# x scaled by its norm on VectorE before it is turned, and the columns of three modulations moved

## What is computed

```python
h = modulate(rms_norm(x, g_pre), shift, scale)   # h * (1 + scale) + shift
y = sublayer(h)
x = x + gate * rms_norm(y, g_post)
```

## Time and profile before

| | |
|---|---|
| median of 3 runs | 1044.78 us (1044.73 to 1045.03) |
| profiled execution, its own time | 1045.76 us |
| its span in the profile | 1044.0 us |
| busy share: PE, PEld, DVE, ACT, POOL | 98%, 86%, 75%, 52%, 7% |
| HBM read | 239.30 MB, 230 GB/s over the span |
| granted TensorE clock, mean | 0.996 |

### The profile page before, as it was taken

The page is one execution under the profiler, slowest core; times in us unless marked ns, Lnnn a source line. Parts: engine busy times, 40 slices in busy tenths (PEclk is TensorE's granted clock), DMA queues, the critical chain, the costliest instruction groups (busy, mean ns, idle before and its releaser), DMA issues.

```text
span 1044.0 us, 17276 instructions
## 1 busy us (share of the span) xinstructions
PE 1020.3 (98%) x7098; PEld 898.2 (86%) x7099; DVE 785.7 (75%) x1162; ACT 538.5 (52%) x706; POOL 74.8 (7%) x79
## 2 busy tenths in 40 slices
PE   6999999999999999999999999999999999999997
PEld 3677799889988999887989899899999689999995
DVE  2457798768878888866968778761787689878786
ACT  4443644344446457765545445454763565544543
POOL 0000000000000000000720000000790000000000
PEclk9999999999999999999999999999999999999999
DMA  9999699887997997003988777723344277555511
GB/s 339 384 369 353 220 348 357 316 318 279 336 330 258 277 376 287 1 5 125 390 300 314 273 285 281 228 86 117 122 141 158 67 249 235 168 196 185 179 41 41
DMA packets 131226, 243.56 MB, mean 233 GB/s; under 512 B 6521, under 2 KB 97228, under 8 KB 125004
## 3 DMA queue, kind: packets, MB, share of 16 engines
q1 hardware_dynamic: 126640, 238.77, 65.1%
q10 hardware_dynamic: 4507, 3.69, 1.3%
HBM read 239.30 MB, written 1.05 MB: 230 GB/s over the span
## 4 chain that ended last, share of the span: by engine, by line
PE 86%; DVE 6%; DMA 2%; ACT 2%; SPq 2%; issue 1%; DVEq 0%; ACTq 0%
PE bank L1898 24%; PE bank L1830 13%; PE bank L1832 12%; PE bank L1831 12%; PE bank L1910 3%; PE bank L1741 2%; DVE wlo L1135 2%; PE bank L1786 1%; SPq L607 1%; PE bank L2175 1%; DMA raw<-in_b_w_in_dram 1%; PE bank L2201 1%; DMA raw<-in_ada_w_dram 1%; PE bank L1768 1%; PE bank L1844 1%
## 5 line engine op out<-in xcount | busy, mean ns | idle before, releaser
L1135 DVE TENSOR_TENSOR wlo<-raw,whi 128x2048 fp32r<-128x2048 f32 (+1 forms) x145 | 331.5, 2291 | 60.0 <-ACT whi L674 58.4
L674 ACT ACTIVATE whi<-raw 128x2048 fp32r<-128x2048 f32 (+1 forms) x145 | 274.9, 1897 | 143.9 <-PE bank L1898 80.5
L1830 PE MATMUL bank<-hcat,whi 128*128 128x256 f32 x1096 | 313.2, 286 | 2.6 <-DVE wlo L1135 2.6
L1831 PE MATMUL bank<-hcat,whi 128*128 128x256 f32 x1096 | 310.7, 284 | 0.0
L1832 PE MATMUL bank<-hcat,wlo 128*128 128x256 f32 x1096 | 310.7, 284 | 0.0
L1830 PEld LDWEIGHTS bank<-hcat,whi 128*128 128x128 f32 x1096 | 209.7, 191 | 9.2 <-DVE wlo L1135 4.0
L1831 PEld LDWEIGHTS bank<-hcat,whi 128*128 128x128 f32 x1096 | 209.8, 191 | 1.4
L1832 PEld LDWEIGHTS bank<-hcat,wlo 128*128 128x128 f32 x1096 | 209.7, 191 | 0.0
L1699 DVE SCALAR_TENSOR_TENSOR cvt<-ut,vec,cvt 128x189 f32<-128x189 f32 (+2 forms) x176 | 68.2, 429 | 22.2 <-ACT cvt L1101 19.8
L1898 PE MATMUL bank<-whi,fhi 128*128 128x512 f32 x240 | 77.0, 402 | 0.0
L1898 PE MATMUL bank<-whi,flo 128*128 128x512 f32 x240 | 74.6, 392 | 0.0
(11 more groups left out here) (405 smaller groups left out, 1700.0 us busy)
## 6 DMA issues: line engine op xcount, KB each, us to landing
raw<-in_ada_w_dram SPq DMA_DIRECT2D x40, 1024.0 KB, 8.0
raw<-in_ff_w_in_dram SPq DMA_DIRECT2D x32, 1024.0 KB, 6.9
raw<-in_ff_w_out_dram SPq DMA_DIRECT2D x32, 1024.0 KB, 6.8
raw<-in_w_ada_dram SPq DMA_DIRECT2D x24, 1024.0 KB, 6.5
raw<-in_w_up_dram SPq DMA_DIRECT2D x22, 1024.0 KB, 5.1
raw<-in_w_in_dram SPq DMA_DIRECT2D x12, 1024.0 KB, 5.4
raw<-in_w_down_dram SPq DMA_DIRECT2D x11, 1024.0 KB, 5.9
raw<-in_ada_w_dram SPq DMA_DIRECT2D x16, 512.0 KB, 11.9
```

The costliest lines, as they stand in the source:

```text
L674: act.activation(whi[:, m % SPL, 0:w], raw[:, pl.nm[m] % RAW, 0:w], ACT.Copy).then_inc(s_hi, 1)
L1135: dve.tensor_tensor(wlo[:, m % SPL, 0:w], raw[:, pl.nm[m] % RAW, 0:w], whi[:, m % SPL, 0:w], ALU.subtract).then_inc(s_lo, 1)
L1830: pe.matmul(dst, wh[:, kt, n], ah[:, kt, :], start=kt == 0, stop=False)
L1831: pe.matmul(dst, wh[:, kt, n], al[:, kt, :], start=False, stop=False)
```

## The change

`norm_tile` no longer builds a diagonal. It multiplies x by its norm on VectorE in four `tensor_scalar` operations of 256 columns each, written into the free tile of `yg`, and counts the semaphore after each. `x_transposes` turns these columns with `pe.transpose` against the identity, two for each step of the semaphore. The wait of VectorE for the earlier transposes is gone, and so is the tile `xd`.

In `update_x`, `mods(between)` moves from behind tile 0 to tile 1, between its additions and the norm of x. The columns of G1A and S1B are turned into bank 6 instead of 7, and by TensorE between the two tiles' transposes of the second and third boundary, before the modulation chunks, after a wait for the gain rows; the columns of S2B stay in bank 7 and are turned after the first tile's transposes of the fourth boundary. In `end_of_y` nothing stands in their place. TensorE waits until the columns have been read before bank 6 is used for a product, and the batch after G1A or S1B waits only for ScalarE's copy, not for the reading of the columns.

```diff
--- before.py
+++ after.py
@@ -109,6 +109,9 @@
 
     def condition(b):
         return int(BATCH[b][0] == 2)
+
+
+    COL_BANKS = {G1A: 6, S1B: 6}
 
     def row_tile(b, i):
         return i + 4 if b == S2 else i
@@ -274,8 +277,6 @@
     gain = sb("gain", [P, D], F32, oS + 16384)
     junk = [t32[:, 2 * i:2 * i + 2, :].rearrange("p k t -> p (k t)") for i in range(4)]
     ident = sb("ident", [P, P])
-
-    xd = sb("xd", [P, 2, P])
     onesm = sb("onesm", [P, P])
     one1 = sb("one1", [P, 256])
     eps = sb("eps", [P, 1])
@@ -483,7 +484,7 @@
     s_sg, s_cp, s_sel = sem("c_silu"), sem("c_padded"), sem("row_selector_ready")
 
     s_yb, s_sqy, s_yg, s_x = sem("y_bank_complete"), sem("y_squares"), sem("y_times_gain"), sem("x_ready")
-    s_sqx, s_xd, s_xT = sem("x_squares"), sem("norm_diagonal"), sem("x_normed_and_transposed")
+    s_sqx, s_xd, s_xT = sem("x_squares"), sem("x_normed"), sem("x_normed_and_transposed")
     s_t, s_hh, s_h = sem("modulated"), sem("h_hi_ready"), sem("h_ready")
     s_diag, s_gmm, s_gain = sem("gain_diagonal"), sem("gain_rows_multiplied"), sem("gain_rows_ready")
     s_v, s_root = sem("half_of_the_squares"), sem("roots_ready")
@@ -562,8 +563,8 @@
     def ada_sums(b, c=0):
 
         if b in TWO_TILES:
-            return ps[ADA_BANK][:, 0:8].rearrange("p (n g) -> p g n", g=2)
-        return ps[ADA_BANK][:, 0:32].rearrange("p (n g c) -> p g n c", g=4, c=2)[:, :, :, c]
+            return ps[COL_BANKS.get(b, ADA_BANK)][:, 0:8].rearrange("p (n g) -> p g n", g=2)
+        return ps[COL_BANKS.get(b, ADA_BANK)][:, 0:32].rearrange("p (n g c) -> p g n c", g=4, c=2)[:, :, :, c]
 
     def ada_rows_ready(eng, b):
         if on_pe(b):
@@ -1203,9 +1204,9 @@
 
                 dve.wait_ge(s_sqx, 4 * e + 2 * tt + 2)
                 r, q = rsqrt(ssx, tt)
-                if e:
-                    dve.wait_ge(s_xT, 4 * e)
-                dve.tensor_scalar(xd[:, tt, :], ident[:, :], r, q, ALU.mult, ALU.mult).then_inc(s_xd, 1)
+                for i in range(4):
+                    n = slice(T * i, T * i + T)
+                    dve.tensor_scalar(yg[:, tt, n], x[:, tt, n], r, q, ALU.mult, ALU.mult).then_inc(s_xd, 1)
 
             def half_of_x(e, tt):
                 dve.wait_ge(s_sqx, 4 * e + 2 * tt + 1)
@@ -1248,13 +1249,13 @@
                     norm_of_y(tt)
                     add(2 * tt)
                     add(2 * tt + 1)
+                    if tt and between is not None:
+                        mods(between)
                     if e is not None:
                         half_of_x(e, tt)
                         norm_tile(e, tt)
                     if tt and late is not None:
                         mods(late)
-                    if not tt and between is not None:
-                        mods(between)
 
             def split_h(o, dh, dl, kts=range(KT)):
 
@@ -1726,7 +1727,9 @@
         def _(pe):
             def ada_bank_free(b):
 
-                if b:
+                if b - 1 in COL_BANKS:
+                    pe.wait_ge(s_row, b)
+                elif b:
                     pe.wait_ge(s_read, b)
 
             def ada_chunk(a):
@@ -1765,7 +1768,7 @@
 
                 sel, w = (sel4[:, :], 8) if b not in TWO_TILES else (sel2[:, :] if on_pe(b) else sel4[:, 0:4:2], 2)
                 for n in range(4):
-                    mm = pe.matmul(ps[ADA_BANK][:, w * n:w * n + w], stage[:, P * n:P * n + P], sel, start=True, stop=True)
+                    mm = pe.matmul(ps[COL_BANKS.get(b, ADA_BANK)][:, w * n:w * n + w], stage[:, P * n:P * n + P], sel, start=True, stop=True)
                 mm.then_inc(s_col, 1)
 
             def gain_row(u, half):
@@ -1780,11 +1783,11 @@
 
             def x_transposes(e, tt, kts=range(KT)):
 
-                pe.wait_ge(s_xd, 2 * e + tt + 1)
                 for kt in kts:
+                    if kt % 2 == 0:
+                        pe.wait_ge(s_xd, 8 * e + 4 * tt + kt // 2 + 1)
                     c0 = T * (kt % 2) + P * tt
-                    mm = pe.matmul(ps[X_BANKS[kt // 2]][:, c0:c0 + P], x[:, tt, kt * P:kt * P + P], xd[:, tt, :],
-                                   start=True, stop=True)
+                    mm = pe.transpose(ps[X_BANKS[kt // 2]][:, c0:c0 + P], yg[:, tt, kt * P:kt * P + P], ident[:, :])
                     if tt and kt % 2:
                         mm.then_inc(s_xT, 1)
 
@@ -1950,6 +1953,9 @@
                     return at_(fhi), at_(flo)
 
                 boundary(2 * f + 1, meanwhile, first)
+                if f == 1:
+
+                    pe.wait_ge(s_read, S1B + 1)
                 ff_in(0, o=o)
                 if f == 1:
                     ada_cols(S2)
@@ -1981,7 +1987,7 @@
 
                 r14 = squares(14)
                 at_ = lambda b: (lambda k, s: b[:, 15 % 3, T * k + s.start:T * k + s.stop])
-                end_of_y(m0 + 30, r14, (at_(fhi), at_(flo)), squares_ready, lambda: ada_cols(ends_at(f, 14)))
+                end_of_y(m0 + 30, r14, (at_(fhi), at_(flo)), squares_ready, lambda: None)
                 ada_chunks(FF_ADA[f][14])
 
             def vectors(n):
@@ -2094,7 +2100,15 @@
                 ffn(0, 1, U_FF0, lambda e: ada_cols(S0B), lambda: ada_chunks(3))
 
             if has("attn"):
-                boundary(2, lambda e: ada_chunks(4))
+                def last_columns(b, u):
+
+                    pe.wait_ge(s_gain, 2 * u + 2)
+                    ada_cols(b)
+                    ada_chunks(4)
+
+                boundary(2, lambda e: last_columns(G1A, U_FF0))
+
+                pe.wait_ge(s_read, G1A + 1)
                 linear_mid(M_KC, gh, gl, o=2)
 
                 for m, t in ((M_VC, 2), (M_KS, 4)):
@@ -2256,14 +2270,15 @@
                     gain_row(U_ATT, 1)
                     pe.wait_ge(s_oh, NPAIR)
 
-                end_of_y(M_BO[2], h_rows(4), h_rows(6), last_heads, lambda: ada_cols(S1B))
+                end_of_y(M_BO[2], h_rows(4), h_rows(6), last_heads, lambda: None)
 
             if has("ffn1"):
-                ffn(1, 4, U_FF1, lambda e: ada_chunks(4))
+                ffn(1, 4, U_FF1, lambda e: last_columns(S1B, U_ATT))
 
             if has("gla"):
 
                 x_transposes(4, 0)
+                ada_cols(S2B)
 
                 pe.wait_ge(s_gain, 8)
                 pe.wait_ge(s_h, 8 * 6)
```

## The result

The changed kernel is slower: 1049.99 us median of 5 runs (1049.64 to 1050.94) against 1044.80 us for the kernel before, ratio 1.0051, 95% interval 1.004 to 1.0063. The forecast was 1047.7 in a range of 1044.9 to 1050.4. The sign held, and so did the mechanism except at the second boundary; the likeliest case was 2.3 us too low, and the time is that of the rival with several falls of the clock (1049 to 1050).

What follows compares the result with a forecast made beforehand. TensorE, 86% of the chain, bounds the kernel, with its waits at five boundaries. Boundaries +2.0 us plus clock +0.9 give +2.9 on the profiled 1045.76, 1048.7, less 0.98 for the median: 1047.7 us, range 1044.9 to 1050.4.

Steps and rivals of the forecast that it cites:

- likeliest case: Whole kernel: boundaries +2.0 us and one clock fall at the first boundary +0.9, 1047.7 us, own range 1046.8 to 1049, chance 0.42.
- rival with several falls of the clock: Fifth and third boundary open idle stretches too, each costing up to 1.2 us more: 1049 to 1050 us, chance 0.16.
- cheap-pieces rival: A piece holds VectorE only 0.20 us, a tile grows by 0.54: sum -1.6 us, 1043.2 us, chance 0.11.
- First boundary, +1.49: VectorE's extra 1.06 us delays the additions, and `mods` of S0B behind four pieces holds ScalarE's modulation: net +1.49 us.
- Second, 0.0: Second boundary: VectorE's second product 0.21 us later, first piece releases ScalarE 0.23 us sooner: net 0.0 us.
- Each tile costs VectorE 1.06 us more: VectorE at each tile: four pieces occupy it 1.32 us where the diagonal took 0.26.
- Third, 0.0: Third boundary, same as the second: product +0.26 us, first piece -0.23, net 0.0 us.
- fourth -0.33: Fourth boundary, TensorE busy throughout: the context product goes on at 694.06 instead of 694.39, net -0.33 us.
- fifth +0.83: Fifth boundary, as the first without `mods`: products back to back, +1.06 - 0.23 = +0.83 us.
- clock stays up, +2.0: Rival: extra VectorE work as in the forecast but no clock fall, +2.0 us, 1046.8 us, chance 0.25.
- The clock, +0.9: One fall of TensorE's clock at the first boundary, after 2.4 us idle: +0.9 us, bounds 0 and 1.4.
- of 3.4 us low between none and all falls on products, and I take 2.1 us: First boundary's clock fall: 2.1 us of low clock hits products, at 0.42 us lost per us.

Runs made afterwards that it cites:

- modulation_early: The changed kernel with `mods` of S0B moved from behind the second tile's four pieces to ahead of them: 1049.43 us, 1.0037 of the kernel before.
- two_pieces: The changed kernel with two pieces of 512 columns a tile instead of four of 256: 1046.45 us, 1.0012 of the kernel before.
- the run with the clock kept up: The changed kernel with matmuls on zeros in TensorE's idle stretches, 8 at the first boundary, 6 at the fifth: 1047.12 us, 1.0020 of the kernel before.
- scaling_only: The kernel before with only the new scaling and transposes, its columns and `mods` where they were: 1054.00 us, 1.0079 of the kernel before.

## Why the prediction was right or wrong

**Prices.** A piece was put at 0.41 us and 0.33 apart; it is 0.41 and 0.32 where GpSimd rests (mean 420 ns over all). From the first piece to ScalarE 0.97 was said, 1.00 measured (326.37 to 327.37 at the second boundary). The cheap-pieces rival fell here.

**First boundary, +1.49:** measured +1.41, by the steps named: additions 1.03 us later against the first tile's norm, `mods` of S0B as ScalarE's releaser. `modulation_early` took 0.70 of it away, `two_pieces` 0.76.

**Second, 0.0:** measured +0.31. The step that failed is "Each tile costs VectorE 1.06 us more" at this place: it took the price of a piece from stretches without GpSimd, and the pieces lie under its mask building, which the 0.34 us diagonal of before did not (it ended at 317.64, the mask's first memset started at 318.62). They took 0.36 us longer than elsewhere, and the third boundary, without GpSimd, has +0.01. The second product came 0.54 us later after the first tile's norm than before, and 0.23 at the third, where both were put at about 0.2.

**Third, 0.0, fourth -0.33, fifth +0.83:** +0.01, -0.26 and +0.81.

The sum of the boundaries was +2.0 and is +2.3 by the rows and +2.1 by the run with the clock kept up, which also gave this rival (clock stays up, +2.0) its time. By the spans alone that run is 1.6 us above the kernel before (medians 1045.0 and 1043.4), the rest of its 2.1 being the part outside.

**The clock, +0.9: the term that was mis-sized.** The step that failed is "of 3.4 us low between none and all falls on products, and I take 2.1 us", together with the choice of one fall. The fall at the first boundary lasted two lengths in the first profile and cost 1.10 us; at the fifth boundary, left to a rival, a second one came in 3 of the 5 kernels' profiles with that idle stretch of 1.5 to 1.6 us, and cost 1.34 or 1.36 us each time (193.17 and 193.19 for 191.83), above the rival's "up to 1.2". The idle stretches had been foreseen, 2.4 and 1.7 us (1.81 and 1.59 measured; "over 2 us" at the first did not come, in part since the columns waited 0.24 us for ScalarE's copy). In the first profile that is +2.46 us of clock for +0.9: of the 2.3 us by which the forecast was low, about 1.5 come from it, 0.3 from the boundaries, and 0.4 from the part outside the span, to which the sum gave nothing.

**The columns** were rightly valued at nothing for themselves (0.8 us was said for their length, 0.92 measured). They had a use that was not named: they fill TensorE's idle time at the second and third boundary. `scaling_only` shows what they keep away, 3 to 4 us, most of it falls of the clock.

**Not settled.** Why a fall lasts 3.4 us in one execution and 6.8 in another. What lengthens the part outside the span. And how much of the sum of falls in one profile is the change: each has up to three more near 58 us, among the attention's matmuls or near 720 us, in kernels that do not differ there.

## What to carry to other kernels

A cheap operation on an engine that is "not the bottleneck" is priced by what stands behind it in that engine's queue: here 1.06 us of scaling ahead of the other tile's product and 1.3 us ahead of a small modulation. Only the piece that releases the next engine needs to be small; the tile that nobody waits for did better in one operation than in four, and small work of others goes behind the first piece, once its inputs are there. When an edit shortens TensorE's work ahead of a wait, look at the length of the idle stretch that opens: at the fifth boundary 1.59 us of it was followed by 1.35 us lost to the low clock, more than the edit's own 0.81 of delay, in three of the five profiles with such a stretch, and with dummy matmuls in the stretch the loss was gone.

## What the runs showed of the hardware

**Idle stretches and the clock.** In the 12 profiles (two of the case, ten of the experiments) TensorE stood idle for 1.5 to 1.94 us ahead of a second tile's turning 14 times, at the first, second, third and fifth boundary, and 12 times the granted clock fell to 0.50, the 1.2 GHz level, between 0.5 us before the turning began and 2 us after; in the other 34 such places, idle for 0.94 us or less, it never did. Ahead of the matmuls near 58 us, with 1.63 to 1.90 us idle in all 12, it fell 4 times. It stayed up after 1.48 us at the fourth boundary of `scaling_only` and after 1.89 us ahead of a modulation chunk near 85 us in `modulation_early`. The length of the gap is thus not all of it. Other falls came with TensorE busy all the time, among the attention's matmuls. The Trainium skill (TensorE: Matmul & The Clock Gate, PE-mode transpose) says that transposes don't count as work for the clock as matmuls do; transposes follow at the boundaries and matmuls at 58 us, which would agree, but no run here changed that alone.

**VectorE beside GpSimd.** The four pieces took 1.74 or 1.75 us under GpSimd's memsets and selects in four profiles and 1.38 without. With one operation of 1024 columns in the same place it was GpSimd's memset that was stretched, from 0.31 to 0.68 us, while VectorE's 0.81 us stayed.
